# Latent attention of the second block: the turning of the probabilities by 32x32 squares on VectorE and two transfers per head

## The reference

```python
sc = einsum('bqhd,bkhd->bhqk', qblk, kf) * scale
sc = where(kpos[None, :] <= qpos[:, None], sc, -inf)
p = softmax(sc, axis=-1)
o = einsum('bhqk,bkhd->bqhd', p, vf)
...
return concatenate([h_ml, h_mla], axis=-1) @ w_out
```

## Time and profile before

| | us |
|---|---|
| median of three runs (1535.6 to 1542.16) | 1538.43 |
| the profiled execution | 1539.2 |
| its span in the profile | 1537.4 |
| TensorE (PE) busy in the span | 1507.9 |
| VectorE (DVE) busy | 1123.2 |
| ScalarE (ACT) busy | 749.0 |
| GpSimd (POOL) busy | 626.4 |

### The profile page before, as it was taken

The page is one execution under the profiler, slowest core; times in us unless marked ns, Lnnn a source line. Parts: engine busy times, 40 slices in busy tenths (PEclk is TensorE's granted clock), DMA queues, the critical chain, the costliest instruction groups (busy, mean ns, idle before and its releaser), DMA issues.

```text
span 1537.4 us, 20424 instructions
## 1 busy us (share of the span) xinstructions
PE 1507.9 (98%) x7106; PEld 1244.4 (81%) x7106; DVE 1123.2 (73%) x1860; ACT 749.0 (49%) x1259; POOL 626.4 (41%) x280
## 2 busy tenths in 40 slices
PE   9999999999999999999999999999999999999998
PEld 7888888778888877888888888777778888888887
DVE  5689999987874445777667769777744897677774
ACT  6554233454552344755444336454763745445444
POOL 3454444333334432243344635341533344444451
PEclk9999999999999999999999999999999999999999
DMA  5343333355543323333333133322103333333321
GB/s 209 96 124 96 96 98 96 93 158 145 164 151 96 96 79 113 97 110 110 98 97 99 57 87 95 92 70 69 35 22 97 143 117 94 99 96 110 98 94 55
DMA packets 46179, 155.74 MB, mean 101 GB/s; under 512 B 5124, under 2 KB 9348, under 8 KB 45832
## 3 DMA queue, kind: packets, MB, share of 16 engines
q1 hardware_dynamic: 45072, 150.95, 31.5%
q10 hardware_dynamic: 1016, 3.61, 0.7%
HBM read 147.20 MB, written 7.35 MB: 101 GB/s over the span
## 4 chain that ended last, share of the span: by engine, by line
PE 85%; DVE 7%; issue 3%; ACT 3%; DMA 1%; POOL 1%; SPq 0%; DVEq 0%; ACTq 0%; POOLq 0%
PE bank L706 83%; DMA w_raw<-in_stream 1%; DVE x_sq L2285 0%; DMA dn_raw<-in_stream 0%; DVE cq_rstd L2221 0%; PE bank L1299 0%; ACT w_hi L1522 0%; DVE bias L2367 0%; ACT dn_first L1816 0%; POOL w_lo L578 0%; DVE bank L2431 0%; POOL res L675 0%; PE bank L1472 0%; PE bank L1115 0%; DVE dn_raw L2641 0%
## 5 line engine op out<-in xcount | busy, mean ns | idle before, releaser
L578 POOL TENSOR_TENSOR w_lo<-w_raw,w_hi 128x1024 fp32r<-128x1024 f32 x191 | 471.9, 2480 | 517.7 <-ACT w_hi L1522 517.5
L706 PE MATMUL bank<-a_hi,w_hi 128*128 128x512 f32 (+1 forms) x1120 | 445.1, 397 | 2.7 <-DVE a_lo L3187 1.7
L706 PE MATMUL bank<-a_hi,w_lo 128*128 128x512 f32 (+1 forms) x1120 | 431.5, 385 | 0.0
L706 PE MATMUL bank<-a_lo,w_hi 128*128 128x512 f32 (+1 forms) x1120 | 431.1, 385 | 0.0
L1522 ACT CAST w_hi<-w_raw 128x1024 fp32r<-128x1024 f32 x199 | 204.7, 1047 | 181.9 <-DMA w_raw<-in_stream 181.8
L706 PEld LDWEIGHTS bank<-a_hi,w_hi 128*128 128x128 f32 x1120 | 210.5, 188 | 49.9 <-issue 3.9
L706 PEld LDWEIGHTS bank<-a_lo,w_hi 128*128 128x128 f32 x1120 | 210.6, 188 | 45.4 <-issue 3.4
L706 PEld LDWEIGHTS bank<-a_hi,w_lo 128*128 128x128 f32 x1120 | 210.4, 188 | 42.3
L590 POOL TENSOR_TENSOR dn_rest<-dn_raw,dn_second 128x1024 fp32r<-128x1024 f32 x39 | 93.7, 2428 | 249.5 <-DVE dn_rest L2660 249.5
L706 PE MATMUL bank<-dn_rest,f_hi 128*128 128x512 f32 x364 | 141.6, 389 | 0.0
L1816 ACT CAST dn_first<-dn_raw 128x1024 fp32r<-128x1024 f32 x54 | 55.7, 1049 | 157.8 <-DVE dn_raw L2641 157.8
(11 more groups left out here) (434 smaller groups left out, 2797.7 us busy)
## 6 DMA issues: line engine op xcount, KB each, us to landing
w_raw<-in_stream SPq DMA_DIRECT2D x199, 512.0 KB, 3.6
dn_raw<-in_stream SPq DMA_DIRECT2D x56, 512.0 KB, 3.6
p_parts<-d_parts SPq DMA_DIRECT2D x8, 640.0 KB, 5.0
d_turned<-p_parts SPq DMA_DIRECT2D x32, 160.0 KB, 3.2
res<-in_xT ACTq DMA_DIRECT2D x1, 2048.0 KB, 9.8
out_y<-res_tok SPq DMA_DIRECT2D x8, 256.0 KB, 2.0
x_raw<-in_xT SPq DMA_DIRECT2D x3, 512.0 KB, 9.0
mem_raw<-in_memT SPq DMA_DIRECT2D x1, 1024.0 KB, 12.5
```

Source lines behind the costliest of these rows:

```text
L578: nc.gpsimd.tensor_tensor(w_lo[:, j, :], w_raw[:, j, :], w_hi[:, j, :].bitcast(F32), ALU.subtract).then_inc(w_lo_done, 1)
L706: return nc.tensor.matmul(o, l, r, start=start, stop=stop)
```

## The change

The latent attention is turned as the first block's is. ACT takes the exponentials of unit `n` into one of four buffers (`l_probs`) from one of three banks (4, 5, 6) and scales them in place by the inverse row sum; DVE turns them by 32x32 squares into `l_parts`, one unit later; SP writes each head's squares to HBM in two pieces (query blocks 0 to 2, then 3) and reads them back in four transfers into `l_turned`, between the loads of the weight ring; PE multiplies a head at a time (20 product instructions, 128 value columns of the head's pair, of which half are kept), at the end of iteration `4h + 7` for head `h`. ACT and DVE split the kept half of bank 2 into `mix_hi` and `mix_lo` head by head. The products of the last head come behind six steps of the third chunk of W_out. PE's first scores in bank 6 wait for nothing, and its first value step no longer waits for the gate output. At the end of the program DVE's last operations are in another order (`end_add` is split in two; the output of token block 2 goes ahead of the last block's additions). Buffers of the W_out input and the number of row-sum columns are moved to fit.

```diff
-        o_rows = [at(f"o_rows{p}", [P, TB, P], o) for p, o in enumerate((C0 + 26624, C0, C0 + 4096, C0 + 8192))]
+        l_probs = [at(f"l_probs{qb}", [P, (qb + 1) * P], o)
+                   for qb, o in enumerate((B0 + 32768, TMP0 + 11264, G0 + 30848, TMP0 + 9216))]
+        l_parts = at("l_parts", [P, RING, TRIANGLE, PART], TMP0 + 4096)
+        l_turned = at("l_turned", [P, RING, TRIANGLE, PART], B0)
...
+            def rows_back(head, turned):
+                rows = p_parts[head].rearrange("(g i) (h n) -> h i g n", g=RING, h=RING)
+                for h in range(RING):
+                    sp.dma_start(turned[PART * h:PART * h + PART, :, :, :].rearrange("i g k j -> i g (k j)"), rows[h]
+                                 ).then_inc(sems["p_landed"], 16)
...
-            for c in range(CH["FF1"] + UPS[0] + 4, CH["FF2"] + 4):
+            for c in range(CH["FF1"] + UPS[0] + 4, CH["OA"] + 5):
+                ring(c)
+
+            def latent_out(h, done, k):
+                sp.wait_ge(sems["pT_ready"], 4 * (MLA_G + h) + done)
+                sp.wait_ge(sems["p_stored"], 16 * (HEADS + 2 * h + done - 3))
+                sp.dma_start(p_parts[HEADS + h].rearrange("p (g k j) -> p g k j", g=RING, k=TRIANGLE)[:, :, k, :],
+                             l_parts[:, :, k, :]).then_inc(sems["p_stored"], 16)
+
+            def latent_back(h):
+                sp.wait_ge(sems["p_stored"], 16 * (HEADS + 2 * h + 2))
+                if h == 0:
+                    sp.wait_ge(sems["gates_turned"], 1)
+                else:
+                    sp.wait_ge(sems["pv_done"], 4 * MLA_G + h)
+                rows_back(HEADS + h, l_turned)
+
+            rings_at = {6: (CH["OA"] + 5,), 7: (CH["OA"] + 6,), 8: (CH["OA"] + 7,), 9: (CH["WO"],), 14: (CH["WO"] + 1,),
+                        20: (CH["WO"] + 2,), 26: (CH["WO"] + 3,)}
+            for n in range(4 * MLA_HEADS):
+                if n % 4 == 2:
+                    latent_out(n // 4, 3, slice(0, part_of(3, 0)))
+                if n % 4 == 3:
+                    latent_out(n // 4, 4, slice(part_of(3, 0), TRIANGLE))
+                    latent_back(n // 4)
+                for c in rings_at.get(n, ()):
+                    ring(c)
+            for c in range(CH["WO"] + 4, CH["FF2"] + 4):
...
-                if k == 0:
+                if k == 0 and tb > 0:
                     pe.wait_ge(evac_dve, o - DVE_FROM)
...
             def latent_scores(n):
-                pe.wait_ge(sems["p_ready"], U0 + n - 1)
-                mla_score(MLA_G + n // 4, n % 4, ps[4 + n % 2][:, 0:(n % 4 + 1) * P]).then_inc(sems["s_ready"], 1)
-
-            def latent_turn(n):
-                pe.wait_ge(sems["p_ready"], U0 + n + 1)
-                pe.wait_ge(sems["pT_copied"], 4 * XH + n)
-                for kb in range(n % 4 + 1):
-                    r = slice(kb * P, (kb + 1) * P)
-                    m = nc.tensor.transpose(ps[6][:, r], probs[:, n % 2, r], ident)
-                m.then_inc(sems["pT_ready"], 1)
-
-            def latent_values(n):
-                h, nk = n // 4, n % 4 + 1
-                pe.wait_ge(sems["pT_copied"], 4 * XH + n + 1)
-                if n % 8 == 0:
-                    pe.wait_ge(sems["o_ready"], MLA_G + n // 8)
-                else:
-                    pe.wait_ge(sems["o_scaled"], n)
-                for kb in range(nk):
-                    m = mm(ps[2][:, 0:MLA_V], probsT[:, n % 2, kb * P:(kb + 1) * P],
-                           v_mla[kb // 2][:, kb % 2, h * MLA_V:(h + 1) * MLA_V], kb == 0, kb == nk - 1)
+                if n >= 3:
+                    pe.wait_ge(sems["p_ready"], U0 + n - 2)
+                mla_score(MLA_G + n // 4, n % 4, ps[4 + n % 3][:, 0:(n % 4 + 1) * P]).then_inc(sems["s_ready"], 1)
+
+            def latent_values(h):
+                pe.wait_ge(sems["p_landed"], 16 * RING * (HEADS + h + 1))
+                pe.wait_ge(sems["o_ready"], MLA_G + h)
+                pair = slice(P * (h // 2), P * (h // 2) + P)
+                for qb in range(TB):
+                    for kb in range(qb + 1):
+                        m = mm(ps[2][:, qb * P:(qb + 1) * P].rearrange("p (g j) -> p g j", g=RING),
+                               v_mla[kb // 2][:, kb % 2, pair], l_turned[:, :, part_of(qb, kb), :], kb == 0, kb == qb)
                 m.then_inc(sems["pv_done"], 1)
-
-            def pair_turn(p):
-                pe.wait_ge(sems["o_scaled"], 8 * p + 8)
-                for qb in range(TB):
-                    m = nc.tensor.transpose(ps[2][:, qb * P:(qb + 1) * P], o_rows[p][:, qb, :], ident)
-                m.then_inc(sems["o_turned"], 1)
...
             for n in range(4 * MLA_HEADS):
                 if n + 2 < 4 * MLA_HEADS:
                     latent_scores(n + 2)
-                turning = n >= 8 and n % 8 == 1
-                if n >= 8 and n % 8 == 2:
-                    latent_values(n - 2)
                 ml_hook(n)
-                if turning:
-                    pair_turn(n // 8 - 1)
-                latent_turn(n)
-                if n >= 1 and not turning:
-                    latent_values(n - 1)
+                if n % 4 == 3 and n >= 7:
+                    latent_values(n // 4 - 1)
                 ml_turns(n)
-            latent_values(4 * MLA_HEADS - 1)
-            pair_turn(MLA_HEADS // 2 - 1)
...
-                        pe.wait_ge(sems["pT_copied"], 4 * (XH + MLA_HEADS))
+                        pe.wait_ge(sems["p_ready"], 4 * (MLA_G + MLA_HEADS))
...
-                    pe.wait_ge(sems["o_ready"], MLA_G + k - ML_HEADS + 1)
+                    pe.wait_ge(sems["o_ready"], MLA_G + 2 * (k - ML_HEADS) + 2)
...
+            for i in range(6):
+                wo_step(2, i)
+            latent_values(MLA_HEADS - 1)
             for j in range(WO_WHOLE):
-                for i in range(6 if j < 2 else 0, KB):
+                for i in range(6 if j < 3 else 0, KB):
...
             def latent_exps(n):
                 act.wait_ge(sems["s_masked"], U0 + n + 1)
-                act.wait_ge(sems["pT_ready"], U0 + n - 1)
-                act.wait_ge(sems["p_inv"], U0 + n - 1)
-                r = slice(0, (n % 4 + 1) * P)
-                A.activation(probs[:, n % 2, r], ps[4 + n % 2][:, r], ACT.Exp, bias=negmax[:, n % 2:n % 2 + 1],
-                             scale=-1.0, accum_out=rowsum[:, n % 2:n % 2 + 1]).then_inc(sems["p_ready"], 1)
-
-            def latent_turned(n):
-                act.wait_ge(sems["pT_ready"], U0 + n + 1)
-                act.wait_ge(sems["pv_done"], U0 + n - 1)
-                r = slice(0, (n % 4 + 1) * P)
-                A.copy(probsT[:, n % 2, r], ps[6][:, r]).then_inc(sems["pT_copied"], 1)
-
-            def pair_hi(p):
-                act.wait_ge(sems["o_turned"], p + 1)
-                A.copy(mix_hi[ML_HEADS + p], ps[2][:, :]).then_inc(sems["o_hi"], 1)
+                if n >= 8:
+                    act.wait_ge(sems["p_inv"], U0 + n - 7)
+                if n >= 4:
+                    act.wait_ge(sems["pT_ready"], U0 + n - 3)
+                A.activation(l_probs[n % 4][:, :], ps[4 + n % 3][:, 0:(n % 4 + 1) * P], ACT.Exp,
+                             bias=negmax[:, n % 2:n % 2 + 1], scale=-1.0, accum_out=rowsum[:, n % 8:n % 8 + 1]
+                             ).then_inc(sems["p_ready"], 1)
+
+            def latent_scaled(n):
+                act.wait_ge(sems["p_inv"], U0 + n + 1)
+                A.activation(l_probs[n % 4][:, :], l_probs[n % 4][:, :], ACT.Copy, scale=rowinv[:, n % 8:n % 8 + 1]
+                             ).then_inc(sems["p_scaled"], 1)
+
+            def latent_hi(h):
+                r = slice(MLA_V * (h % 2), MLA_V * (h % 2) + MLA_V)
+                act.wait_ge(sems["pv_done"], U0 + h + 1)
+                A.copy(mix_hi[ML_HEADS + h // 2][r, :], ps[2][r, :]).then_inc(sems["o_hi"], 1)
 
             latent_exps(0)
             latent_exps(1)
             open_gate(0)
             round_to(CH["VM"])
             for n in range(4 * MLA_HEADS):
-                if n >= 8 and n % 8 == 1:
-                    pair_hi(n // 8 - 1)
-                latent_turned(n)
+                if n % 4 == 0 and n >= 8:
+                    latent_hi(n // 4 - 2)
+                latent_scaled(n)
                 if n + 2 < 4 * MLA_HEADS:
                     latent_exps(n + 2)
                 ml_hook(n)
-            pair_hi(MLA_HEADS // 2 - 1)
             for n in range(4 * MLA_HEADS, ML_END):
+                if n == 4 * MLA_HEADS:
+                    latent_hi(MLA_HEADS - 2)
                 ml_hook(n)
+            latent_hi(MLA_HEADS - 1)
...
             def latent_inverse(n):
                 dve.wait_ge(sems["p_ready"], U0 + n + 1)
-                b = slice(n % 4, n % 4 + 1)
-                V.reciprocal(rowinv[:, b], rowsum[:, n % 2:n % 2 + 1]).then_inc(sems["p_inv"], 1)
-
-            def latent_scaled(n):
-                dve.wait_ge(sems["p_inv"], U0 + n + 1)
-                dve.wait_ge(sems["pv_done"], U0 + n + 1)
-                e = MLA_V * (n // 4 % 2)
```

(79 more changed lines are left out.)

4 lines of the change are left out of this document (2 added, 2 removed).

## The result

The median of 20 runs is 1542.4 us (1540.0 to 1545.9) against 1539.3 us of the kernel before (20 runs): ratio 1.0024, 95% interval 1.0017 to 1.0030. The change costs 3.1 us, less than the 0.5% that the prediction called no change; it had forecast 1526, with a range that ends at 1536 and 0.21 for no change.

What follows compares the result with a forecast made beforehand. PE, busy 1507.9 of 1537.4 us, was taken as the bound. Terms -3.0 - 3.5 - 8.9 + 3.7 - 0.85 = -12.6 took 1539.2 to 1526.6, median 1526; range 1518 to 1536.

Steps and rivals of the forecast that it cites:

- Start: Stage start: PE's waits for the first exponentials and the gate output go, iteration 2 begins earlier; -3.0 us.
- Iterations 2 to 9: 33.5 us stretch: PE loses turns and value products, gains head 0, with 1.1 kept back for DVE; -3.5 us.
- Iterations 10 to 31: 73.4 us stretch: unit-by-unit waits go, floor 59.1, taken as 64.5; -8.9 us, bounds 60 and 69.5.
- The transfers: Each head's round through HBM: 8.5 us against a cover of 9.9, so 0 us while covered.
- ring loads: Weight loads queued behind the read-backs on SP, placed near the iterations that free their slots: 0 us, bound 1.5.
- Rival 3: HBM round closes a loop: PE waits for landings before each head's products, 3.3 x 6 = 20 us; 1546, chance 0.08.
- Behind the last unit: Stage end: head 7's products move behind the last unit, with a bare 1.4 us hop; +3.7 us.
- The last us: Program end: the last addition follows PE directly instead of three DVE operations; -0.85 us, bounds 0 and -0.9.
- (1): ACT or DVE becomes the bound; iterations 10 to 31 take 69.5, 2 to 9 save 2.0; 1532, chance 0.20.
- (2): Given back at the seams: half clock +1.5, late ring loads +1.5, chunk 4 of W_out +2; 1531, chance 0.10.
- (4): No change: extra ACT and DVE work in iterations 10 to 31 ends up in series, +11.5; 1537, chance 0.05.
- The sentence that put 1.5 us on a wait that is moved: Start: a wait moved rather than removed keeps its half-clock price, making that term -1.5 us.

Runs made afterwards that it cites:

- e12: Changed kernel with late casts, head 7's values first, residual scalings cut to 32 columns, transfers of heads 1 to 7 left out: 1528.3 us, ratio 0.9934.
- e9: Changed kernel with one added wait on GpSimd alone, two remainders starting only after VectorE's negm_diag of head 1: 1537.7 us, ratio 0.9989.
- e2: Changed kernel with two of ScalarE's ring casts, and GpSimd's remainders behind them, moved from iterations 10 and 11 to 12 and 13: 1536.2 us, ratio 0.9978.
- e5: Changed kernel with both the two later casts and the ring loads issued ahead of the read-backs: 1532.6 us, ratio 0.9960.
- e3: Changed kernel with SP's ring loads of iterations 7 and 20 issued ahead of their head's read-back (20 becomes 19): 1538.4 us, ratio 0.9991.
- e1: Changed kernel without the HBM transfers of heads 1 to 7 and their waits, all heads reading head 0's tile: 1538.2 us, ratio 0.9991.
- e6: As e5, with head 7's value products ahead of the six products of the third output chunk: 1532.1 us, ratio 0.9955.

## Why the prediction was wrong

**Start, -3.0: right in size.** From the first to the fifth scores 14.50 us became 9.84, -4.7; of that 1.2 comes back at once as PE's wait of 1.19 us for the fourth value chunk's remainder, which I had put ahead of the fifth scores. The granted clock is 1.00 from the first to the 13th scores. (A slip in the term: 1037.0 less 1033.8 is 3.2, not 3.3.)

**Iterations 2 to 9, -3.5: measured -1.3** (32.16 us for 33.50). PE stood 2.4 us in it: the 1.19, and 0.41 and 0.82 for DVE's `v_ml`, where I had kept 1.1 back for DVE. Start and this stretch together are -6.0 for -6.5.

**Iterations 10 to 31, -8.9: the step that failed.** It was +6.3: 79.5 us where I had 64.5. The work was priced well: PE 59.0, ACT 59.1 and DVE 53.4 in my sum, 60.4, 58.3 and 50.9 in e12. What failed is the step "the busiest engine fills 90% now ... with looser coupling I take 64.5". It took every duration of DVE from a trace in which `negm_diag` happened to miss GpSimd and a hold of the same size fell on two copies, with 0.82 us of waiting for PE behind them, and it added no term for work of both. Of the 15.0 us, 6.6 go when only GpSimd is held back (e9) and 8.1 with the casts moved (e2), the fallen clock behind the stall in it. The ring load's place takes another 2.4 (e5 less e2). Another 2.0 go in e12 against e5, with the scalings and the transfers cut, and 2.5 are left against my 64.5. For these I have rows but no run: in e12 PE stands 6.4 us for `sT`, 2.3 of it behind operations that GpSimd holds, and the mean granted clock is 0.95, so 6.7 us of the stretch passed at the lower level. Bounds of 60 and 69.5 would have held e5, not this kernel.

**The transfers, 0 while covered; ring loads 0, bound 1.5.** The round was indeed shorter than I had it, 7.2 for 8.5 us. The ring load's place was mis-sized: 2.4 us in this stretch (e5 less e2; 3.2 for e3 alone, a part of it A's) against a bound of 1.5. And the cover was taken as a constant. It is the way from a late unit to PE's need, and it shrinks just when ACT has been held up. One wait of 3.0 came of it, not six. Rival 3 did not act: no wait per head, and e5, with all transfers in place, stands 0.6 us for them. In the profile e1 is 2.9 us shorter than e3, but their medians are the same, so a smaller cost of the transfers stays open.

**Behind the last unit, +3.7: +4.3** (131.8 us from the first W_out product for 127.5). The bare wait is the 1.40 us forecast, and it could be hidden (e6). Half clock was left over from the waits ahead, and the first two W_out products took 0.77 and 0.63 us instead of 0.47 and 0.39: about the rest. PE had no wait for chunk 4.

**The last us, -0.85: -0.78,** and 0.80 when undone.

**Rivals.** (1) named the right stretch for the wrong reason: neither ACT nor DVE was full, 58.8 and 56.4 of 79.5. (2) had the ring loads at about half their price, and the half clock, whose price no run gives alone. (3) came nearest in time, 1546, by a mechanism that did not act. (4)'s cost in series did not come either. None of the four had the mechanism that decided.

Half clock was itself a term of that stretch: a mean of 0.90 over 79.5 us between the levels 1.2 and 2.4 GHz is 15.9 us at the lower one, where before it was none. It follows the two long waits and, at the end of the stage, two of 0.79 and 1.65 us for `sT` (0.50 from 1142 to 1146, shown above). Behind the first and the second long wait:

```profile
1082.00:1086.00 4.00, 1.76 (x7) 1.68 (x8) 3.58 (x13) 2.63 (x6) 0.07 (x1) 0.65 0.43 123
1086.00:1090.00 4.00, 4.00 (x13) 2.77 (x12) 3.26 (x11) 3.66 (x12) 1.97 (x2) 0.50 0.46 113
...
1130.00:1134.00 4.00, 4.00 (x25) 4.00 (x24) 1.96 (x6) 3.52 (x10) 0.00 (x0) 0.62 0.65 201
```

The sentence that put 1.5 us on a wait that is moved was about the start, where the clock did not fall; it fell here.

## What to carry to other kernels

Before a change that lets engines run ahead, list the VectorE operations with two SBUF inputs and its copies within SBUF (3.86 us for 0.75 in the kernel before), and GpSimd's work near them: their durations in the old trace hold only for the old phase, and a short one in front of a critical product can grow from 0.9 to 4.8 us. A wait added to GpSimd can be the repair. When transfers join a queue, ask for each load that stands behind them whose list waits for it, and issue it in the time in which the queue waits anyway.
